# Gate pieces, mixed tiles and early output rows in the last step of each layer; a query turn moved behind a gate piece

## The reference

```python
for layer in (0, 1):
    h = rms_norm(x, norm)
    q, k, v = h @ w_qkv                  # 16 heads in 4 groups; layer 1: three patterns p each
    o_p, lse_p = banded_attention(q, k, v)
    o = sum_p softmax_p(lse_p) * o_p     # layer 0: one p, coefficient 1/denominator
    mixed = o * silu(h @ w_gate)         # (1024, 1024)
    x = x + mixed @ w_out
return rms_norm(x, final_norm)
```

## Time and profile before

| | |
|---|---|
| time, median of 3 runs (lowest, highest) | 1429.42 us (1428.33, 1431.09) |
| the profiled execution's own time | 1429.45 us |
| its span, first to last instruction | 1427.7 us |
| mean granted TensorE clock | 0.963 of full speed |
| PE busy | 1317.5 us, 92% |
| DVE busy | 732.4 us, 51% |
| ACT busy | 635.2 us, 44% |
| POOL busy | 394.3 us, 28% |
| chain of waits that ended last | PE 84%, DVE 6%, DMA 4% |

### The profile page before, as it was taken

The page is one execution under the profiler, slowest core; times in us unless marked ns, Lnnn a source line. Parts: engine busy times, 40 slices in busy tenths (PEclk is TensorE's granted clock), DMA queues, the critical chain, the costliest instruction groups (busy, mean ns, idle before and its releaser), DMA issues.

```text
span 1427.7 us, 24896 instructions
## 1 busy us (share of the span) xinstructions
PE 1317.5 (92%) x8938; PEld 1228.0 (86%) x8938; DVE 732.4 (51%) x2225; ACT 635.2 (44%) x1767; POOL 394.3 (28%) x443
## 2 busy tenths in 40 slices
PE   5899999999399997999999999899999999994996
PEld 5898998987399897999979999899999799983996
DVE  5545453544732524555436764356654367646625
ACT  6344453636511434544436554346444365545011
POOL 2211051330501111131212823106722128223210
PEclk9999999999799998999999999999999999995998
DMA  5011021121435211011021311212310212134522
GB/s 191 17 30 45 23 61 66 45 82 42 159 102 186 76 36 46 15 36 28 18 79 47 87 57 32 59 34 75 93 29 17 80 47 76 54 91 104 148 89 118
DMA packets 101080, 97.32 MB, mean 68 GB/s; under 512 B 30688, under 2 KB 87520, under 8 KB 100960
## 3 DMA queue, kind: packets, MB, share of 16 engines
q1 hardware_dynamic: 100960, 95.73, 22.5%
HBM read 79.46 MB, written 16.25 MB: 67 GB/s over the span
## 4 chain that ended last, share of the span: by engine, by line
PE 84%; DVE 6%; DMA 4%; ACT 2%; POOL 2%; issue 2%; SPq 1%; DVEq 0%; POOLq 0%; ACTq 0%
PE j_bank L1096 58%; PE s_bank L1199 8%; PE o_bank L1232 7%; PE t_bank L1211 6%; PE j_bank L1178 3%; DVE ht_lo L1690 1%; DMA qk<-mix_dram 1%; DVE ht_lo L1568 1%; DMA w_raw<-in_w_out 1%; DMA gate<-in_positions 1%; PE s_bank L1096 1%; PE o_bank L1096 1%; ACT ht_hi L1380 1%; DVE w_lo L1499 1%; SPq L800 1%
## 5 line engine op out<-in xcount | busy, mean ns | idle before, releaser
L1096 PE MATMUL j_bank<-w_hi,ht_hi 128*128 128x384 f32 (+1 forms) x1328 | 454.1, 342 | 15.5 <-DVE ht_lo L1568 7.1
L1096 PE MATMUL j_bank<-w_lo,ht_hi 128*128 128x384 f32 (+1 forms) x1328 | 441.8, 333 | 0.0
L1096 PE MATMUL j_bank<-w_hi,ht_lo 128*128 128x384 f32 (+1 forms) x1328 | 441.4, 332 | 0.0
L970 POOL TENSOR_TENSOR w_lo<-w_raw,w_hi 128x768 fp32r<-128x768 f32 (+1 forms) x60 | 101.0, 1683 | 695.8 <-ACT w_hi L1307 694.7
L1096 PEld LDWEIGHTS j_bank<-w_hi,ht_hi 128*128 128x128 f32 x1328 | 254.6, 192 | 27.8 <-issue 20.3
L1096 PEld LDWEIGHTS j_bank<-w_lo,ht_hi 128*128 128x128 f32 x1328 | 255.0, 192 | 0.0
L1096 PEld LDWEIGHTS j_bank<-w_hi,ht_lo 128*128 128x128 f32 x1328 | 254.2, 191 | 0.0
L1316 ACT ACTIVATE probs<-probs,stat 128x256 f32<-128x256 f32 (+1 forms) x512 | 230.6, 453 | 31.1 <-DVE stat L1531 29.5
L1526 DVE CUSTOM_DVE_ANT_0 probs<-s_bank,masks 128x128 f32<-128x128 f32 (+1 forms) x448 | 142.4, 354 | 135.2 <-PE t_bank L1211 131.5
L722 ACT COPY probs_t<-t_bank 128x256 f32<-128x256 f32 (+1 forms) x128 | 57.9, 452 | 311.4 <-PE o_bank L1232 306.2
L1199 PE MATMUL s_bank<-ks,qs 128*128 128x256 f32 (+1 forms) x1024 | 144.1, 284 | 4.6 <-DVE ks L1585 4.3
(11 more groups left out here) (159 smaller groups left out, 1645.1 us busy)
## 6 DMA issues: line engine op xcount, KB each, us to landing
w_raw<-in_w_qkv SPq DMA_DIRECT2D x64, 384.0 KB, 3.3
coef<-coef_dram SPq DMA_DIRECT2D x96, 128.0 KB, 2.9
w_raw<-in_w_gate SPq DMA_DIRECT2D x32, 256.0 KB, 3.3
mix_dram<-xr SPq DMA_DIRECT2D x12, 512.0 KB, 3.9
w_raw<-in_w_out SPq DMA_DIRECT2D x16, 384.0 KB, 3.5
qk<-mix_dram SPq DMA_DIRECT2D x12, 512.0 KB, 5.1
xr<-in_x SPq DMA_DIRECT2D x8, 512.0 KB, 7.5
out<-xr SPq DMA_DIRECT2D x8, 512.0 KB, 2.7
```

The lines of the kernel that those rows point to most:

```text
L970: pool.tensor_tensor(quarter(n, q, 1), raw_quarter(n, q), quarter(n, q, 0).bitcast(F32), ALU.subtract).then_inc(w_lo_done["p"], 1)
L1096: last = pe.matmul(to, a(x_, kt), b(y_, kt), start=(start and kt == kts[0] and x_ == y_), stop=(stop and kt == kts[-1] and x_ == 1))
```

## The change

The gate pieces of a layer's last step go to slots 0, 4, 8 and 12. The second half of the output weights' first job is split behind slot 14 instead of slot 8, and SP's loads that stand with it move too. The coefficients of the last group's first tile are turned and copied in slot 13 instead of 11. The six loaded tiles are no longer split in the step: ACT and DVE do so behind it, mixed with the coefficients of the second tile, and ACT's silu of the last gate stands behind the second tile instead of in pair 6. SP issues the loads of tiles 3, 4 and 5 behind the step's slots. The early rows run tile by tile (all seven rows with tile 0, then all with tile 1, and so on), each tile as soon as it is split; `coef_turn` 1 stands behind the first tile. POOL waits for silu only in front of the multiplication by it. Apart from that, in pair 12 of steps 6, 9 and 12 (the next step is the first pattern of a group) the fill of queries stands behind the first gate piece instead of in front of it.

```diff
@@ -73,7 +73,7 @@
             JOBS.append(("gate", _layer, _s.g))
-            _slots.append((JOBS[-1], [0, 2, 4, 6] if _s.last else [12, 13, 14, 15]))
+            _slots.append((JOBS[-1], [0, 4, 8, 12] if _s.last else [12, 13, 14, 15]))
         for _job, _pieces in _slots:
@@ -84,7 +84,7 @@
         elif _s.last:
-            _at += [(3, _now[0] + 1, (0,)), (5, _now[0] + 1, (1,)), (8, _now[0] + 1, (2, 3))]
+            _at += [(3, _now[0] + 1, (0,)), (5, _now[0] + 1, (1,)), (14, _now[0] + 1, (2, 3))]
         else:
@@ -136,10 +136,10 @@
 MIX_AT = {0: 8, 1: 8}
-SPLIT_MIX = [8, 9, 10, 11, 14, 15]
 EARLY = 7
 SPARE = [2, 3, 4, 5, 6]
-END_FIRST, END_EXP, END_LAST, END_TURN, END_COPY = 8, 9, 10, 11, 11
+EARLY_ORDER = [0, 1, 2, 3, 6, 4, 5]
+END_FIRST, END_EXP, END_LAST, END_TURN, END_COPY = 8, 9, 10, 13, 13
 def mix_items(s, rs=(0, 1)):
@@ -307,7 +307,7 @@
     work = []
-    if a == 0 and not by_class(s):
+    if (a == 0 and not by_class(s)) or (a == 12 and not s.last and by_class(STEPS[s.t + 1])):
         work, pieces = pieces[:1], pieces[1:]
@@ -906,14 +906,13 @@
                                     mix_load(layer, k)
-                            for k in range(3, MIX_LOADS):
-                                if slot == max(SPLIT_MIX[k - 3] + 1, 12 if k > 3 else 0):
-                                    mix_load(layer, k)
                             if slot == END_COPY:
                 last = steps[-1]
+                for k in range(3, MIX_LOADS):
+                    mix_load(layer, k)
                 coef_store(last, 1)
@@ -1019,7 +1018,6 @@
                 pool.wait_ge(ot_stored, 4 * s.t + 2 * r + 2)
-                pool.wait_ge(silued, groups_before(s.t) + 1)
                 for _, half, p in mix_items(s, (r,)):
@@ -1033,6 +1031,7 @@
                         opened = half_blocks(gate_of(s.layer, s.g)[:, r, :], s.layer, half)
+                        pool.wait_ge(silued, groups_before(s.t) + 1)
                         end_link(pool.tensor_tensor(into, into, opened, ALU.mult), done)
@@ -1133,27 +1132,25 @@
                 return bank_[:, 0:out_width(0)]
-            def early_row(layer, k):
+            def early_rows(layer, kt):
                 job = ("out", layer, 0)
                 last_step = LAYER_STEPS[layer][-1]
-                if k == 0:
-                    for half in range(2):
-                        weights_half(job, half)
-                    pe.wait_ge(mix_lo, layer * MIX_TILES + MIX_LOADS)
-                    pe.wait_ge(mix_hi, layer * MIX_TILES + MIX_LOADS)
-                if k not in SPARE:
-                    free_bank(PIECE, piece_empty, job + (k,))
-                elif k < 4:
-
-                    pe.wait_ge(biased, UNITS * (last_step.t + 1))
-                elif k < 6:
-
-                    pe.wait_ge(ot_stored, 4 * (last_step.t + 1))
-                else:
-                    wait_turn_emptied(pe, (last_step.t, UNITS - 1))
-                a, b, _ = operands(job, k)
-                products(out_bank(layer, k), a, b, range(MIX_LOADS), True, False)
+                if kt % 4 == 0:
+                    weights_half(job, kt // 4)
+                pe.wait_ge(mix_lo, layer * MIX_TILES + kt + 1)
+                pe.wait_ge(mix_hi, layer * MIX_TILES + kt + 1)
+                for k in EARLY_ORDER:
+                    if kt == 0 and k not in SPARE:
+                        free_bank(PIECE, piece_empty, job + (k,))
+                    elif kt == 0 and k < 4:
+                        pe.wait_ge(biased, UNITS * (last_step.t + 1))
+                    elif kt == 0 and k < 6:
+                        pe.wait_ge(ot_stored, 4 * (last_step.t + 1))
+                    elif kt == 0:
+                        wait_turn_emptied(pe, (last_step.t, UNITS - 1))
+                    a, b, _ = operands(job, k)
+                    products(out_bank(layer, k), a, b, [kt], kt == 0, False)
             def later_row(layer, r, k):
@@ -1278,9 +1275,9 @@
                     times_v(last, u)
-                for k in range(EARLY):
-                    early_row(layer, k)
-                    if k == 1:
+                for kt in range(MIX_LOADS):
+                    early_rows(layer, kt)
+                    if kt == 0:
                         coef_turn(last, 1)
@@ -1449,15 +1446,7 @@
                             w_hi(SPLIT_BEHIND.get(s.t, []))
-                        if s.last and SPLIT_MIX[0] - 1 in pair:
-                            silu(s)
-
-                            act.wait_ge(piece_full, PIECE.filled(last_piece(JOB[("gate", layer, GROUPS - 1)])))
                         for slot in pair:
-                            if s.last and slot in SPLIT_MIX:
-                                k = SPLIT_MIX.index(slot)
-                                act.wait_ge(mix_back[k % 3], 16 * (layer * 2 + k // 3 + 1))
-                                mix_split(layer, k, mix_in[k % 3])
                             if slot == (1 if layer == 0 else 3) and before is not None and before.ends_group:
@@ -1465,7 +1454,14 @@
                     empty_turn(last, u)
-                den_exp(last, 1)
+                act.wait_ge(piece_full, PIECE.filled(last_piece(JOB[("gate", layer, GROUPS - 1)])))
+                for k in range(MIX_LOADS):
+                    act.wait_ge(mix_back[k % 3], 16 * (layer * 2 + k // 3 + 1))
+                    mix_split(layer, k, mix_in[k % 3])
+                    if k == 0:
+                        den_exp(last, 1)
+                    if k == 1:
+                        silu(last)
                 for r in range(2):
@@ -1854,16 +1850,17 @@
                                 coef_copy(s, 0)
-                            if s.last and slot in SPLIT_MIX:
-                                k = SPLIT_MIX.index(slot)
-                                mix_split(layer, k, mix_in[k % 3])
                 last = steps[-1]
                 coefs_first(last, 1)
+                mix_split(layer, 0, mix_in[0])
+                store_ot(last, 1, 1)
                 coefs_last(last, 1)
-                store_ot(last, 1, 1)
-                coef_copy(last, 1)
+                for k in range(1, MIX_LOADS):
+                    mix_split(layer, k, mix_in[k % 3])
+                    if k == 2:
+                        coef_copy(last, 1)
                 mix_split(layer, MIX_LOADS, ot[out_region(last)][:, 0, :])
```

## The result

The changed kernel takes 1390.87 us (median of 4 runs, 1389.62 to 1395.92) against 1429.28 for the kernel before: a ratio of 0.9736, 95% interval 0.971 to 0.9763. It is faster by 38.4 us where 47.4 were forecast. Measured once more beside the last experiments, the ratio was 0.9724 (0.9701 to 0.9747). The profiled execution took 1391.8 us, with a span of 1390.0 where it was 1427.7. Lines of the changed kernel stand some lines earlier: PE's products are L1095, scores L1196, fills L1175, turns L1208, `coef_turn` L1240.

A forecast was written before the change was run, and what follows sets the result against it. PE was taken as the bound, busy 92% of the span, with idle time and slow clock to win. Gains of 19.8 (layer 0), 13.2 (layer 1) and 14.7 (query turns) sum to 47.7 us off 1429.45: 1382, range 1370 to 1399.

The forecast's parts named there:

- The tail up to the first tile: From coef_turn 0 to the first mixed tile in each layer's last step: 12.5 us in layer 0, 10.5 in layer 1.
- layer 0's early rows: Layer 0, tile by tile at 3.65 us each; 40.3 us from coef_turn 0 to the second mark, now 51.6.
- The two things said of PE's idle time: Ahead of the early rows: PE idle for two thirds of the tail to tile 0, and some 8 us in all.
- Pair 2: Last steps, its fill uncovered: 6.2 us in layer 0 and 5.7 in layer 1, some 2.7 us of it idle.
- "6.2 + 8.6" and "5.7 + 7.9": Pair 2 plus pair 4 in layers 0 and 1, first terms of 39.0 and 34.4 us up to coef_turn 0.
- Layer 1's end: Tile 7's wait ends last, by some 3 us: 42.7 us from coef_turn 0 to the second mark, now 48.98.
- The residual rows and the half clock behind it hide under this: Layer 1's tail: weights, residual rows and half clock add nothing beyond the wait for tile 7; layer 1 wins 13.2 us.
- The query turn: Pair 12 of steps 6, 9, 12: 4.9 us won each, 14.7 together; second piece waits 0.2 us for ACT's copy.
- Rival A: Layer 1's tail: DVE and POOL go in turns, layer 1 gains only 4.5 us; time 1391, chance 0.18.
- B: Last steps: the tail's idle only replaces the old one, the query turns alone win 14.7 us; 1415, chance 0.10.
- C: Pair 12: the query turn wins nothing, its second piece waiting for ACT and the weights' load; 1397, chance 0.05.
- D: Early rows: PE waits for every tile in turn (load, split high, split low), adding 80 us; 1462, chance 0.03.

The follow-up runs named there:

- e3: Changed kernel with the early rows one row after another again and coef_turn 1 ahead of them: 1414.76 us, 0.9882 of the kernel before.
- e4: Changed kernel with DVE's split of tile 6 between the halves of its products of tile 7, not ahead of them: 1389.09 us, 0.9715.
- e6: Changed kernel without DVE's low parts of mixed tiles 1 to 5 in layer 1 (left out of the computation): 1387.24 us, 0.9686.
- e9: The changed kernel once more, unaltered, beside the last three experiments: 1393.36 us, 0.9724 of the kernel before.
- e5: Changed kernel with gate pieces in pairs 2, 4, 8, 12 instead of 0, 4, 8, 12: 1393.37 us, 0.9738.
- e1: Kernel before with only the query turn moved behind the first gate piece of pair 12 (steps 6, 9, 12): 1417.9 us, 0.9907.
- e7: Changed kernel with gate pieces in pairs 2, 4, 8, 12, tile 6's split between DVE's product halves, last coefficients' copy one split earlier: 1387.86 us, 0.9694.
- e10: As e7, with SP issuing the store and loads of the last half's coefficients ahead of the load of tile 5: 1391.43 us, 0.9703.
- e8: As e7, with the second half of the output weights split late, behind the first mixed tiles, in both layers: 1390.27 us, 0.9714.
- e11: As e10, with layer 1's gate pieces in pairs 0, 2, 6, 10 and its coefficients' turn at slot 11: 1394.16 us, 0.9729.
- e12: As e11, with the second half of layer 1's output weights loaded and split behind the first mixed tiles: 1389.21 us, 0.9691.

## Why the prediction was right, and where it was not

The time lies in the range, 9 us above the value. The mechanisms were those named, with one step wrong.

**The tail up to the first tile and layer 0's early rows** came out as worked: 12.0 us for 12.5 and 10.6 for 10.5, then 40.3 for 40.3 from `coef_turn` 0 to the mark, with the slow clock on tile 0 that the sum had let stand. Nothing waits between the tiles of layer 0. The two things said of PE's idle time up to there, two thirds of it and some 8 us in all, don't agree with each other; it was 5.4 of 12.0 us in layer 0 and 5.9 of 10.6 in layer 1.

**Pair 2** lasted 6.26 us (6.2 foreseen) with 2.8 us idle (2.7). The step that failed is the next one: "6.2 + 8.6" and "5.7 + 7.9" priced pair 4 at full clock. It took 10.3 and 11.2 us, at a granted clock of 0.51 over the first 5 us in layer 1. The sum had priced the half clock behind one idle stretch, that ahead of tile 0, and not behind this one. In this execution that is 1.7 + 3.3 = 5.0 of the 10.0 us by which the profiles fall short of 47.7, the largest part. In layer 0 the 1.7 us are the mechanism's: five profiles with this order have 10.3 us there (the changed kernel, e3, e4, e6, e9), and e5, with a piece in pair 2, has 8.7. In layer 1 the same five have 11.2, 9.6, 11.2, 8.0 and 9.6, so the 3.3 us are the high end of 0.1 to 3.3, and partly chance. In e6 the whole stretch from the score of pair 2 to `coef_turn` 0 took 34.9 us, the forecast's 34.4 nearly.

**Layer 1's end** was the wait foreseen, ht_lo ahead of tile 7, but 5.0 us instead of 3. POOL started at 7.6 us behind `coef_turn` 0 as said, took 23.4 instead of 22, and everything behind moved by it; DVE's products took 8.7 us as said. That makes 44.4 for 42.7 (its own terms add up to 42.8), a term 1.7 too small. "The residual rows and the half clock behind it hide under this" was wrong for what follows the mark: 2.35 us were lost there, because the wait for tile 7 is followed by half a clock of its own.

**The query turn**: 4.4, 4.6 and 4.4 us for 4.9. In pair 12 the second piece waits 0.4 us for ACT's copy where 0.2 was set. The three and the drift between them give 13.8 for 14.7. (Two pieces of 5.4 and a fill of 0.4 are 11.2, not 11.3.) Another 1.3 us lie between layer 0's mark and the first score of layer 1, see the last section.

Added up: 47.7 - 2.2 (layer 0) - 5.3 (layer 1) - 2.35 (behind it) - 0.9 - 1.3 + 2.0 (start) = 37.7.

**Rival A** named 1391 us, and that is the number, by another way. Its mechanism is there. In the stretch where DVE splits tiles 1 to 5 (1280.53 to 1292.4) five of POOL's operations take 11.35 us, 2.27 each where they take some 1.42 alone (e6), and a split takes 2.3 to 2.4 in place of 1.22. One after the other they would take 2.64 us, so where they meet they go nearly in turns. The Trainium skill, "SBUF — State Buffer", "Who interferes with whom", says that such operations hold a shared port for a whole instruction each; in this stretch the trace comes close to that. What the rival had wrong is the extent: there are five splits and not twelve, so POOL lost 5 x 0.85 = 4.2 us, where the rival priced 8.6. The 4.2 are what e6 gave back (4.1 on POOL, 4.2 at the mark). Only 1.4 of them were missing from the forecast, which had put POOL at 22 us. That the time is still the rival's 1391 is a coincidence of numbers: most of what is missing is slow clock in other places, which the rival had not priced.

**Rivals B, C and D**: B is near what e3 shows once rows go one after another; C falls by e1; of D, waits ahead of every tile, there is no trace in either layer (0.35 us ahead of tile 1 in layer 1, then none up to tile 7).

Still open is whether the last waiting can be had. e4, e6 and e7 brought the 5.0 us ahead of tiles 6 and 7 down to 3.6, 2.1 and 3.6, and e10 has 4.5 ahead of tiles 5 and 7. Each time another link stood just behind: first DVE's products, then the coefficients in SP's queue, then tile 5 in the same queue.

## What to carry to other kernels

Where a piece of work that hides waits is moved, price both ends: what its old place hid (here a fill of 2.8 us in pair 2, and another, for POOL's rotation, in pair 0), and the slow clock that may follow each gap that opens (here between 0.1 and 3.3 us more behind 2.8, from one execution to the next). With the splits behind the step, a tail that starts with the first of several late tiles, looping over tiles outside and rows inside, was worth 21 to 23 of 38 us. What it would bring with the splits left in the step, or what the moved gate pieces bring with the old tail, was not run. And once the tail is tile by tile, the slowest tile's chain ends it; in e8 an earlier first tile brought nothing.

## What was not expected of the hardware

**The same wait is followed by either clock.** Up to here e9 and e6 have the changed kernel's order, and in all three PE waits 2.80 us for the fill of pair 2 in layer 1. Windows of 5 us behind that wait, first in e9, then in e6:

```profile
1237.18:1242.18 5.00, 5.00 (x29) 4.12 (x30) 3.42 (x14) 2.72 (x8) 0.00 (x0) 0.67 0.31 80
```

```profile
1239.59:1244.59 5.00, 5.00 (x35) 4.24 (x36) 4.10 (x15) 3.43 (x11) 0.00 (x0) 1.00 0.33 80
```

The changed kernel's own window had 0.51 and 25 matmuls, these have 0.67 and 29, and 1.00 and 35. Pair 4 took 11.2, 9.6 and 8.0 us by it. The waits for tile 7 in e7 and e10 are alike too, and so is the work behind them. Windows of 6 us behind it, first in e7, then in e10:

```profile
1307.66:1313.66 6.00, 6.00 (x25) 6.00 (x26) 4.28 (x8) 0.00 (x0) 1.08 (x1) 0.72 0.77 264
```

```profile
1307.40:1313.40 6.00, 5.97 (x34) 5.97 (x35) 4.08 (x8) 0.00 (x0) 1.11 (x1) 1.00 0.89 305
```

A wait of 2.74 us was followed by a mean of 0.72, one of 2.72 by 1.00, and 25 matmuls went by in one window and 34 in the other: 78.9 us to the end against 77.4. Here the work in front of the wait is not the same, and it may be that which decides: e4 goes with e7 (0.72), e11 and e12 go with e10 (1.00). A wait of 1.88 us between the layers was followed by 1.00 in the kernel before and by 0.72 in the changed one, in code that is the same; that accounts for the 1.3 us lost there. From layer 0's mark to the first score of layer 1, where PE's order is the same in every version, the fourteen profiles have 124.2 to 128.9 us (e10 the least, 124.4 in the kernel before, 125.7 in the changed one). Behind the waits for tile 7 of 5.0 and 6.7 us the clock was halved (0.54; 0.53 in e5), behind the 1.4 us of the kernel before it was not. A gain of 1 or 2 us in one profile can be this alone, which is also why several of the versions above can't be told apart.

**Small operations of DVE suffer as well.** In the changed kernel one addition of 128x16 beside POOL's work takes 1.39 us, the next 0.18. Two rows of DVE, then the POOL operation beside the first:

```profile
1277.52 1.39 DVE L1645 TENSOR_TENSOR comb<-comb 128x16 f32<-128x16 f32 x1
1278.94 0.18 DVE L1646 TENSOR_TENSOR comb<-comb 128x16 f32<-128x16 f32 x1
```

```profile
1277.36 1.52 POOL L1030 TENSOR_TENSOR xr<-xr 128x512 f32<-128x512 f32 x1
```

The first ends at 1278.91, 0.03 us behind the end of POOL's operation: it lasted as long as what was left of that one, whatever its own size.
